# Forget gate in two steps of the plan, latent transposes ahead of the retention's rope, retention scores inside the gate's product

## The reference

```python
# first block, hgrn2_mixer: 8 heads of 128
log_f = jnp.logaddexp(jnp.log(lb), jnp.log1p(-lb) + jax.nn.log_sigmoid(f_logit))
k = -jnp.expm1(log_f)
bc = jnp.cumsum(chunks(log_f), axis=3)
# attn[t, s] = q[t] k[s] exp(b[t] - b[s]), o = attn @ i + (q exp(b)) @ state
# first block, nsa_mixer: three softmaxes (compressed, selected, window) per head,
# each times its gate, then @ v, summed over the three

# second block, token_mixing
(ret_q, ret_k, ret_v, ret_g, mla_qa, mla_kva, d_q, d_k, d_v, gate_logits) = split(h @ w_in)
# retention: q, k = apply_rope(...)
scores = einsum('bcnhd,bcmhd->bchnm', qc, kc) * intra_decay
o = rms_norm(scores @ v + (q * q_decay) @ state)      # y_ret = silu(ret_g) * o
# latent_attention
q = (rms_norm(c_q_raw, q_norm) @ wq_b)                # 8 heads of 64 + 32 (rope)
kv = (rms_norm(c_kv, kv_norm) @ wkv_b)
p = softmax(mask((q_nope k_nope + q_rope k_rope) * scale));  y_mla = p @ v
```

## Time and profile before

| | |
|---|---|
| median of 3 runs | 2228.26 us |
| the profiled execution, its own time | 2229.36 us |
| its span (first to last instruction) | 2227.6 us |
| TensorE matmul busy | 2119.8 us (95%) |
| VectorE busy | 1422.3 us (64%) |
| ScalarE busy | 1044.7 us (47%) |
| DMA | 357.75 MB, mean 161 GB/s |

### The profile page before, as it was taken

The page is one execution under the profiler, slowest core; times in us unless marked ns, Lnnn a source line. Parts: engine busy times, 40 slices in busy tenths (PEclk is TensorE's granted clock), DMA queues, the critical chain, the costliest instruction groups (busy, mean ns, idle before and its releaser), DMA issues.

```text
span 2227.6 us, 27633 instructions
## 1 busy us (share of the span) xinstructions
PE 2119.8 (95%) x11555; PEld 1815.9 (82%) x11555; DVE 1422.3 (64%) x1790; ACT 1044.7 (47%) x1460; POOL 109.1 (5%) x121
## 2 busy tenths in 40 slices
PE   6999999999899999899999899999998999999998
PEld 5988887988787888687888788878886878877887
DVE  4756776756777766565775566666665566755665
ACT  4544535444545544444544345554544453544543
POOL 0100010100011100000000000010000000000000
PEclk9999999999899999999999999999999999999999
DMA  7463235363235655435545355555544354553552
GB/s 251 120 203 117 95 117 176 112 203 117 76 123 174 232 190 181 137 108 165 174 167 180 115 206 189 198 204 193 190 143 157 115 168 168 184 169 128 195 189 95
DMA packets 192692, 357.75 MB, mean 161 GB/s; under 512 B 8316, under 2 KB 85176, under 8 KB 192568
## 3 DMA queue, kind: packets, MB, share of 16 engines
q1 hardware_dynamic: 189688, 345.51, 46.4%
q0 software_dynamic: 2880, 10.49, 1.4%
HBM read 354.92 MB, written 1.05 MB: 160 GB/s over the span
## 4 chain that ended last, share of the span: by engine, by line
PE 80%; DVE 11%; ACT 4%; issue 2%; POOL 1%; DMA 1%; SPq 0%; POOLq 0%; ACTq 0%; DVEq 0%
PE bank L1906 15%; PE bank L1912 14%; PE bank L1902 14%; PE bank L1944 11%; PE bank L1948 6%; DVE raw_r L2404 4%; PE bank L1966 3%; PE bank L2086 2%; PE bank L1983 2%; ACT high L2195 2%; PE bank L1957 2%; PE bank L1926 2%; PE bank L1929 2%; PE bank L1932 2%; PE bank L2004 1%
## 5 line engine op out<-in xcount | busy, mean ns | idle before, releaser
L2404 DVE TENSOR_TENSOR raw_r<-raw,high 128x2048 fp32r<-128x2048 f32 x304 | 685.9, 2273 | 77.7 <-ACT high L2195 76.5
L2195 ACT ACTIVATE high<-raw 128x2048 fp32r<-128x2048 f32 x304 | 573.9, 1895 | 235.0 <-PE bank L1912 194.3
L1902 PE MATMUL bank<-high,units_r 128*128 128x512 f32 (+1 forms) x1616 | 647.9, 401 | 9.6 <-ACT units_r L2212 4.5
L1906 PE MATMUL bank<-high,units_r 128*128 128x512 f32 (+1 forms) x1616 | 634.9, 393 | 20.5 <-DVE units_r L2428 12.2
L1912 PE MATMUL bank<-raw_r,units_r 128*128 128x512 f32 (+1 forms) x1616 | 433.5, 390 | 1.6 <-DVE raw_r L2404 1.6
L1906 PEld LDWEIGHTS bank<-high,units_r 128*128 128x128 f32 x1616 | 305.6, 189 | 86.5 <-DVE units_r L2428 16.7
L1902 PEld LDWEIGHTS bank<-high,units_r 128*128 128x128 f32 x1616 | 305.1, 189 | 74.0 <-issue 8.3
L1912 PEld LDWEIGHTS bank<-raw_r,units_r 128*128 128x128 f32 x1616 | 304.5, 189 | 66.2 <-DVE raw_r L2404 3.1
L1944 PE MATMUL bank<-units_r,high 128*128 128x512 f32 x1152 | 288.3, 392 | 2.6 <-DVE units L2756 2.6
L1944 PEld LDWEIGHTS bank<-units_r,high 128*128 128x128 f32 x1152 | 208.6, 189 | 40.9 <-issue 3.0
L1948 PEld LDWEIGHTS bank<-units_r,raw_r 128*128 128x128 f32 x1152 | 157.2, 191 | 11.2
(11 more groups left out here) (253 smaller groups left out, 2161.0 us busy)
## 6 DMA issues: line engine op xcount, KB each, us to landing
raw<-in_ffn_w_dram SPq DMA_DIRECT2D x132, 1024.0 KB, 5.1
raw<-in_w_in_dram SPq DMA_DIRECT2D x108, 1024.0 KB, 5.1
raw<-in_w_out_dram SPq DMA_DIRECT2D x24, 1024.0 KB, 4.9
raw<-in_cross_wkv_dram SPq DMA_DIRECT2D x16, 1024.0 KB, 5.2
raw<-in_w_branch_dram SPq DMA_DIRECT2D x12, 1024.0 KB, 4.9
raw<-in_cross_wq_dram SPq DMA_DIRECT2D x8, 1024.0 KB, 6.3
raw<-in_cross_wo_dram SPq DMA_DIRECT2D x8, 1024.0 KB, 5.0
raw<-in_w_in_dram SPq DMA_DIRECT2D x4, 832.0 KB, 4.5
```

What stands on the lines that cost most here:

```text
L1902: pe.matmul(o, h.high(k0 + k)[:, span], p.hi[k][:, cols], start=start and k == 0, stop=False, skip_group_check=True)
L1906: pe.matmul(o, h.low(k0 + k)[:, span], p.hi[k][:, cols], start=False, stop=False, skip_group_check=True)
L2195: done = act.activation(high, raw, ACT.Copy)
L2404: done = dve.tensor_tensor(low, raw, high.bitcast(F32), ALU.subtract)
```

## The change

Three edits, none of which adds or removes an arithmetic instruction:

1. The step "forget" becomes two. "softplus" holds the ScalarE part; "forget" holds the VectorE part. `gate_f()` now yields once at its start, issues softplus for both halves with a rest behind each, and then forget for both halves with a rest behind each. The banks of the product f are given back behind the VectorE half, as before.
2. In `mla_in()` the `yield` between "latent" and `latent_turn` is gone.
3. In `ret()` the product of the gate is opened first (`gates_of`, banks taken), two of its four `tok` tiles are let out, then come the `ret_scores`, then a plain `yield`, then the rest of the product and the gate's silu. The `yield "rest"` behind the scores is gone.

```diff
--- before.py
+++ after.py
@@ -1136,8 +1136,12 @@
                 if l == 1:
                     t2 = U.take()
                     bounds = [a[:, 4 * hg:4 * hg + 4] for a in (LNLB, LN1M, NEG_LNLB)]
+                yield "rest"
                 for q, (b, pr) in enumerate(fb):
-                    do("forget", name=H, q=q, need=pr, bank=b, k_=k_, tl=tl, tc=tc, t2=t2, bounds=bounds)
+                    do("softplus", name=H, q=q, need=pr, bank=b, tl=tl, t2=t2, bounds=bounds)
+                    yield "rest"
+                for q, (b, pr) in enumerate(fb):
+                    do("forget", name=H, q=q, bank=b, k_=k_, tl=tl, tc=tc, bounds=bounds)
                     B.give(b, ("logf", H, q))
                     yield "rest"
                 if l == 1:
@@ -1420,7 +1424,6 @@
                 kr_made.append(r)
                 B.give(b, ("latent", M), r)
                 latents.append(tmp)
-            yield
             for t, tmp in enumerate(latents):
                 b = B.take()
                 M = f"{N}.l{t}"
@@ -1604,13 +1607,9 @@
                 t_made += plan.turn(f"{N}.rT{t}", qs.ap[:, t * 512:t * 512 + 512], [rows_of[t]], [rT], t)
             U.give(qs, ("turnp", f"{N}.rT1", 0))
             yield
-            rg = U.take()
-            g_made = []
-            for t, (b, pr) in enumerate((yield from proj(1024, 512))):
-                s = plan.silu(f"{N}.rg{t}", [pr], rg.ap[:, t * 512:t * 512 + 512], b.ap, rg.after)
-                B.give(b, s)
-                g_made.append(s)
-                yield
+            gates_of = proj(1024, 512)
+            yield next(gates_of)
+            yield next(gates_of)
             s0, s1 = U.take(), U.take()
             r3 = h3(rT.ap, 4)
             s_made = []
@@ -1623,7 +1622,14 @@
                     B.give(b, ("decayed", R))
                     s_made.append(("decayed", R))
             U.give(rT, ("ret_scores", R))
-            yield "rest"
+            yield
+            rg = U.take()
+            g_made = []
+            for t, (b, pr) in enumerate((yield from gates_of)):
+                s = plan.silu(f"{N}.rg{t}", [pr], rg.ap[:, t * 512:t * 512 + 512], b.ap, rg.after)
+                B.give(b, s)
+                g_made.append(s)
+                yield
             yr = U.take()
             for t in range(2):
                 b = B.take()
@@ -2316,7 +2322,7 @@
             act.activation(rr, rr, ACT.Sin, bias=0.0, scale=1.0).then_inc(*mark(s.expd, ("sines",)))
             act.preload_act_table_set(TAB)
 
-    def forget(name, q, need, bank, tl, t2, bounds, **_):
+    def softplus(name, q, need, bank, tl, t2, bounds, **_):
         sl = slice(q * 512, q * 512 + 512)
         if q == 0:
             act.preload_act_table_set(TAB_LN)
@@ -2376,7 +2382,7 @@
 
     tiles = dict(split_high=split_high, turn_put=turn_put, turn_split=turn_split, copy=copy, fold=fold, tanh=tanh, gates=gates, gate_rows=gate_rows, rope=rope, soft_exp=soft_exp, keys=keys,
                  head_squares=head_squares, norm_squares=norm_squares,
-                 post_squares=post_squares, bounds=bounds, angles=angles, forget=forget,
+                 post_squares=post_squares, bounds=bounds, angles=angles, softplus=softplus,
                  log_key=log_key, level_exp=level_exp, latent=latent, glu_split=glu_split)
     tiles["lambda"] = lambda_
     for kind, how in steps:
```

## The result

| | before | changed |
|---|---|---|
| median | 2228.27 us (4 runs, 2227.33 to 2232.01) | 2198.75 us (4 runs, 2195.69 to 2202.65) |
| ratio of the runs | | 0.9865, 95% interval 0.9849 to 0.9881 |
| the profiled execution, its own time | 2229.36 us | 2196.72 us |
| its span | 2227.6 us | 2194.9 us |
| TensorE busy, and idle | 2119.8, 107.8 us | 2104.0, 90.9 us |

The kernel is 29.5 us faster by the medians and 32.6 us between the two profiled executions. Of the 32.7 us between the spans 16.9 are idle time of TensorE (107.8 to 90.9); the other 15.8 are busy time. As no instruction was added or taken, busy time can only shrink by the clock and by how matmuls overlap.

The account below looks back on a forecast made before the run. TensorE's work plus its gaps bounds the kernel; only 107.8 us of gaps and its lower clock can move. Gains of 11.0 + 10.5 + 2.7 + 1.1 + 1.8 = 27.1 from 2229.4 give 2202.3, stated 2202.5 us, range 2193 to 2215.

Parts of the forecast that it names:

- Edit 2: Mixings, latent's transposes: waits of 4.35 and 1.33 us go, a new wait of 2.4 us comes, in each mixing.
- Edit 3: Mixings, retention: the 3.30 us wait of `ret_v` goes in each mixing, with 0.8 us new at later scores.
- The 0.8 us "at the second" score set: Mixings: a new wait of about 0.8 us at the second of the next two retention score sets, in each.
- Edit 1, first heads: First four heads, layer 1 alone: `same`'s wait of 1.76 us falls to 0.75; gain 2.7 us with the clock.
- with the clock's 1.7 us: Layer 1's first heads: the 1.7 us lost to half clock behind the wait ending at 405.94 comes back.
- Edit 1, second heads: Second four heads, with NSA attention woven in: removed waits outweigh new ones, gaining 1.1 us in layer 0, 1.8 in layer 1.
- the long wait: Second heads, each layer: `keys` waits about 3.7 us for `nsa_gate`, with 1.7 us of clock charged behind it.
- Rival "the new 2.4 us wait also lowers the clock": Both mixings: the wait ahead of the latent's transposes loses 1.7 to 3.1 us of clock each; 2207 us, chance 0.15.
- Rival "head gates worse": Second heads: net -6.6 us instead of +2.9 while the mixings gain; 2212 us, chance 0.17.
- Rival "the new waits in the head gates are shorter": Head gates: engines' queues overlap better than counted, up to 18 us more gain, say half; 2193 us, chance 0.10.
- Rival of the PSUM hand-over: Forget's banks held longer, so TensorE waits at eight hand-overs per layer, 0.7 to 2.6 us each; 2241 us, chance 0.05.
- What was to be seen: Signs: no latent-product or `ret_v` waits, latent transposes 2.4 us twice, `keys` 3.7 twice, full clock behind layer 1's first heads.

Follow-up runs that it names:

- edit 2 alone: The kernel before with only the `yield` between latent and `latent_turn` in `mla_in()` removed; 2213.56 us.
- the experiment on edit 3: The kernel before with only the `ret()` change, retention's scores inside the gate's product; 2222.68 us.
- Edit 1 alone: The kernel before with only the forget gate split into softplus and forget steps; 2222.24 us.
- the second profile: The changed kernel run once more with nothing altered; median 2198.43 us.
- the run with the forget late: The changed kernel with an even tile before the latent's transposes, tiles kept in the second heads, and their forget steps one rest later, behind `nsa_gate`; 2195.90 us.
- edits 1 and 2: The changed kernel without the `ret()` change, so retention's scores stay where they were before; 2201.15 us.

## Why the prediction was right, and where it wasn't

The forecast of 2202.5 (2193 to 2215) met 2198.75; faster, as given 0.90. By its steps:

- Edit 2, right in kind and size: the wait of 4.35 us gone, 2.2 us new for 2.4 forecast, 1.33 us gone, in both mixings. What the step missed is that the same `yield` moves the whole softmax stream against the retention; edit 2 alone took 5.1 of the 6.6 us of `ret_v`'s waits.
- Edit 3, wrong in its size beside edit 2. "The wait goes, 3.3 us each time" is true of the sum but I gave it to edit 3. Alone it does remove 6.6 us; beside edit 2 it adds 2.8 us of idle time. The 0.8 us "at the second" score set never came and the new wait was 2.2 for 2.4, so the mixings gained 11.7 and 11.6 where I said 11.0 and 10.5.
- Edit 1, first heads: 1.76 us became 0.69, as forecast. The term "with the clock's 1.7 us" was mis-argued: the experiment on edit 3 shows that at full clock a wait of 1.75 us takes the place of that loss, as long as nothing else changes. In the changed kernel that wait is 0.53 us, and the stretch from 403.48 to the next level's wait (492.41) is 88.93 us for 90.07, so 1.1 us came in place of the 1.7. The rows show that it took two things: VectorE has one split (2.28 us) behind 403.48 where two (4.90) stood, and the clock is at full. With two splits at full clock (edit 3 alone) the way to the level's product is 11.00 us; with one it is 413.24 - 403.48 = 9.76. At 0.83 TensorE was busy for 10.8 of the 10.99 us, so a shorter queue alone would have given next to nothing. The prediction saw that split move into the idle time between the halves, and gave it no price.
- Edit 1, second heads: the long wait is right to 0.2 us (3.55 and 3.73 for 3.7), the third `pv` waited 1.94 for 3.2 and the last 0.25 for 1.0 and 1.1. But I charged the smaller loss of clock, 1.7 us, behind each 3.7. In the changed kernel half clock stood there over 6.8 us at each in the first profile, 3.4 and 6.8 in the second, of which up to 1.8 us lie inside the wait: 2.9 and 2.9 us of loss behind the waits, and 1.7 and 2.5. With the 1.7 behind the third `pv`, charged and come in the first profile only, the six waits of that profile cost 2.9 us less than forecast (10.5 for 13.4) and the clock 2.4 us more (7.5 for 5.1). The two errors cancel, and that the sum is near (6.0 us gained in the first 675 us for 5.6 forecast) is luck to that extent. Edit 1 alone gave 6.9.
- Not in the prediction at all: 3.4 us from stages without an edit. That is most of what the profiled execution was below the forecast (2196.72 for 2202.3, 5.6 us), and it is chance of the execution: the second profile has the falls back and took 2200.66.
- Rival "the new 2.4 us wait also lowers the clock": true in 4 of the 12 times that such a wait stands in the profiles, 1.7 us each. So it isn't an either-or, as I had it, but a cost of 0.6 us on average for each.
- Rival "head gates worse": no. Rival "the new waits in the head gates are shorter": so for three of the six, but the clock took it back. Rival of the PSUM hand-over: not in the changed kernel; seen once, in the run with the forget late.
- What was to be seen was seen: no lines for L2124 and L2161, L2115 twice, L1980 with 3.7, full clock behind the first heads of layer 1, no new gap in the levels.

## What the runs showed of the hardware

I had expected a wait to bring the same fall of the clock each time. Over the 14 profiles, waits of 3.3 us and more (`keys` behind `nsa_gate` in the kernels with edit 1 and two forget steps of the old order, the latent products, `ret_v`) were followed by a stretch at half clock in all 26 cases; the two of 3.1 us in untouched stages in 17 of 28; those of 2.64 and 2.75 us in 10 of 28; those of 2.2 us in 7 of 26; those of 1.75 us at 1130 and 1896 in 11 of 28. Waits of 1.73 us at three other places were followed by none in 42, while one of 1.04 us at `ret_v` was followed by one both times that it stands in the second mixing (edit 2 alone, edits 1 and 2). Each loss, counted over the whole stretch at half clock, which can begin inside the wait, came out as 1.7, 3.4 or 5.1 us. So neither the place nor, below 3.3 us, the length decides by itself. What else does isn't shown.

The Trainium skill (TensorE: Matmul & The Clock Gate, section "HAM oscillation") ties the fall to gaps that are long enough. That agrees with the longest ones here, and not with a 2.64 us wait that fell in 6 profiles of 14 at one and the same place.

Executions of one kernel differ by 8 us (2196.2 to 2204.5) at the same waits, and they line up with their granted clock: 2196.2 at 0.995, 2200.7 at 0.993, 2204.5 at 0.992. And a loss of clock costs only where TensorE is the one that is waited for: 0.0 of 1.7 us at 405.94.

## What to carry to other kernels

Where two streams are woven by yields, a moved or removed `yield` shifts everything behind it against the other stream: look for its gain at every later wait of both streams, and don't add up the edits' own gains. Compare TensorE's idle time, which came out within 0.2 and 0.6 us where the same program ran twice, before the median, which carries several us of clock; and charge the clock behind a wait as a chance, in full only for waits that are long (3.3 us and more here). Covering a wait with more work on one engine helps only if the releasing engine's queue keeps the needed row in front.
